# State-space inputs by four row groups with the power outermost, constants beside the memory's projection, and the angles' rounding constant added by ScalarE

## Time and profile before

| | |
|---|---|
| median of three runs | 4084.74 us |
| the profiled execution, its own time | 4090.44 us |
| its span on the core | 4089.1 us |
| TensorE busy, of the span | 3879.4 us, 95% |
| VectorE / ScalarE / GpSimd busy | 63% / 44% / 36% |
| mean granted TensorE clock | 0.969 of full speed |

### The profile page before, as it was taken

The page is one execution under the profiler, slowest core; times in us unless marked ns, Lnnn a source line. Parts: engine busy times, 40 slices in busy tenths (PEclk is TensorE's granted clock), DMA queues, the critical chain, the costliest instruction groups (busy, mean ns, idle before and its releaser), DMA issues.

```text
span 4089.1 us, 66513 instructions
## 1 busy us (share of the span) xinstructions
PE 3879.4 (95%) x28426; PEld 3308.2 (81%) x28426; DVE 2578.3 (63%) x3605; ACT 1794.3 (44%) x2785; POOL 1480.2 (36%) x701
## 2 busy tenths in 40 slices
PE   6898999999999999989899999999989989999998
PEld 3787888777877887888788888888978878888887
DVE  0435643795368897669678758784555966455457
ACT  1435443654355444445544444443334554333334
POOL 0332443143323440014334444445424434444443
PEclk8998999999999999999999999999689999999999
DMA  9653665345543451024346555556225435454543
GB/s 395 264 215 144 262 242 209 149 175 204 220 154 139 171 191 69 23 105 172 149 165 227 206 217 206 215 197 268 104 94 197 179 130 190 183 196 179 200 177 133
DMA packets 60119, 747.66 MB, mean 183 GB/s; under 512 B 6704, under 2 KB 8880, under 8 KB 16176
## 3 DMA queue, kind: packets, MB, share of 16 engines
q1 hardware_dynamic: 48960, 696.74, 44.7%
q0 software_dynamic: 8800, 44.57, 2.8%
q10 hardware_dynamic: 2064, 2.10, 0.1%
HBM read 726.60 MB, written 16.78 MB: 182 GB/s over the span
## 4 chain that ended last, share of the span: by engine, by line
PE 78%; DVE 12%; ACT 5%; DMA 3%; issue 1%; POOL 0%; another core or an unknown queue 0%; SPq 0%; DVEq 0%; ACTq 0%; POOLq 0%
PE ps L370 42%; PE ps L371 21%; DVE pieces L323 2%; PE ps L3548 2%; DMA ring<-in_ada 2%; PE ps L2229 2%; PE ps L790 2%; ACT pieces L307 2%; DVE r L1173 1%; DVE opa L571 1%; PE ps L1899 1%; DMA s5u<-in_s5bt 1%; PE ps L3578 1%; DVE scr L592 1%; PE ps L644 1%
## 5 line engine op out<-in xcount | busy, mean ns | idle before, releaser
L370 PE MATMUL ps<-opa,pieces 128*128 128x512 f32 x6192 | 2256.0, 407 | 59.4 <-DVE pieces L323 39.6
L341 POOL TENSOR_TENSOR pieces<-ring,pieces 128x1024 fp32r<-128x1024 f32 x539 | 1348.5, 2502 | 2233.9 <-ACT pieces L307 2224.2
L371 PE MATMUL ps<-opa,pieces 128*128 128x256 f32 x6192 | 1741.5, 281 | 0.0
L307 ACT ACTIVATE pieces<-ring 128x1024 fp32r<-128x1024 f32 (+1 forms) x1110 | 1098.4, 1036 | 838.3 <-PE ps L371 837.9
L370 PEld LDWEIGHTS ps<-opa,pieces 128*128 128x128 f32 x6192 | 1174.2, 190 | 355.8 <-issue 41.9
L371 PEld LDWEIGHTS ps<-opa,pieces 128*128 128x128 f32 x6192 | 1179.6, 191 | 9.0 <-issue 5.3
L370 PE MATMUL ps<-opb,pieces 128*128 128x512 f32 x2560 | 910.5, 397 | 18.6 <-DVE pieces L323 13.0
L323 DVE TENSOR_TENSOR pieces<-ring,pieces 128x1024 fp32r<-128x1024 f32 (+1 forms) x571 | 715.0, 1252 | 272.8 <-ACT pieces L307 269.3
L371 PE MATMUL ps<-opb,pieces 128*128 128x256 f32 x2560 | 726.0, 284 | 0.0
L370 PEld LDWEIGHTS ps<-opb,pieces 128*128 128x128 f32 x2560 | 483.4, 189 | 140.2 <-issue 15.3
L371 PEld LDWEIGHTS ps<-opb,pieces 128*128 128x128 f32 x2560 | 484.0, 189 | 0.1
(11 more groups left out here) (425 smaller groups left out, 3478.1 us busy)
## 6 DMA issues: line engine op xcount, KB each, us to landing
ring<-in_up SPq DMA_DIRECT2D x64, 2048.0 KB, 7.7
ring<-in_down SPq DMA_DIRECT2D x64, 2048.0 KB, 7.7
ring<-in_win SPq DMA_DIRECT2D x56, 2048.0 KB, 7.8
ring<-in_ada SPq DMA_DIRECT2D x48, 2048.0 KB, 12.1
ring<-in_wout SPq DMA_DIRECT2D x24, 2048.0 KB, 7.7
ring<-in_evin SPq DMA_DIRECT2D x18, 2048.0 KB, 7.8
ring<-in_evout SPq DMA_DIRECT2D x8, 2048.0 KB, 7.9
ring<-in_xkv SPq DMA_DIRECT2D x8, 2048.0 KB, 7.7
```

Of the source, the lines that this page charges most:

```text
L307: a.do.activation(K.parts_of(p)[0][:, s, :], w[:, s, :], ACT.Copy).then_inc(*K.hi.up((p, h)))
L341: g.do.tensor_tensor(lo[:, s, :], w[:, s, :], hi[:, s, :].bitcast(F), ALU.subtract).then_inc(*K.lo2.up(p))
L370: pe.do.matmul(b[:, 0:512], hi[:, k, :], op[:, 512 * k:512 * k + 512], start=i == 0, stop=False)
L371: t = pe.do.matmul(b[:, 0:256], lo[:, k, :], half(op, 0, k), start=False, stop=i == kt - 1)
```

## The change

The inputs `z5` of an s are computed in one call by all four row groups, with the power r outermost. VectorE's steps therefore wait for whole sets of four. The order of inputs and outputs on TensorE and of the output additions on VectorE is changed. The generators for the columns move from the first quarter's up tiles to the eight tiles of the memory's projection (`xkv`) of layer 0. `row5` is no longer made by `wide5` and matmuls: TensorE transposes the two 128x64 tiles, ScalarE copies the result, and it goes to HBM and comes back in 16 DMAs issued by GpSimd, each of 16 partitions with 16 repeats of 256 bytes. The load of the first table moves with it. ScalarE makes the second of the four angle operations. The pads of table 6 are spread over eight tiles.

```diff
@@ xattn, layer 0 @@
     for n in range(8):
+        if l == 0 and n == 6:
+            pe_s5_rows(K)
         side = pe_xvturn(K, l, n - 5) if n > 4 else None
@@ act_xattn / dve_xattn @@
+    columns = iter(()) if l else act_s5_columns(K)
     for n in range(8):
         act_feed(K, ahead(K, p + n))
+        next(columns, None)
...
+    columns = iter(()) if l else dve_s5_columns(K)
     for n in range(8):
         dve_feed(K, ahead(K, p + n))
         dve_normed(...)
+        for _ in range(1 + (n > 0)):
+            next(columns, None)
@@ pool_xo @@
     pool_feed(K, K.first["xo", l] - 1)
+    if l == 0:
+        pool_s5_first(K)
+        pool_s5_rows(K)
@@ pe_ffn @@
-            if l == 0 and q == 0 and n in (12, 15):
-                pe_s5_rows(K, n // 2 - 6)
@@ act_s5_columns: the four L3135 and the four L3142 go @@
+    a.wait_ge(*K.prod.of("lamT"))
+    a.do.activation(K.lamT, K.bank["lamT"][0:64, 0:256], ACT.Copy).then_inc(*K.act.up("lamT"))
@@ pe_s5_rows @@
+    for c, lam in enumerate((K.lre5, K.lim5)):
+        pe.wait_ge(*K.dve.of(("lam5", c)))
+        t = pe.do.transpose(b[0:64, P * c:P * c + P], lam, K.ident)
@@ new @@
+def pool_s5_rows_back(K):
+    g = K.g
+    g.wait_ge(*K.load["lamT"].of("lamT"))
+    g.wait_ge(*K.tile.of(K.first["up", 0, 0]))
+    for c in range(2):
+        for r in range(4):
+            for q in range(2):
+                at = 32 * r + 16 * q
+                rows = K.D["s5lam"].rearrange("(m r) (c q t) -> r c q m t", r=4, c=2, q=2)[r, c, q]
+                g.do.dma_start(K.row5[c][at:at + 16, :].rearrange("p (m t) -> p m t", m=16),
+                               rows[None].broadcast_to([16, 16, 64])).then_inc(*K.load["row5"].up("row5", 16))
@@ pool_s5_beside @@
     for t in range(2, 128):
+        if t == 4:
+            pool_s5_rows_back(K)
@@ act_s5_pads @@
-        yield
+            if j == 6:
+                yield
+        if j < 6:
+            yield
@@ pool_s5_angle / act @@
-    g.do.tensor_scalar(K.at5, K.aq, 1.0, MAG, ALU.mult, ALU.add).then_inc(*K.gps.up())
-    g.wait_ge(*K.gps.now())
+    g.wait_ge(*K.act.of(("whole5", m)))
     g.do.tensor_scalar(K.at5, K.at5, -MAG, None, ALU.add).then_inc(*K.gps.up())
+def act_s5_whole(K, m):
+    K.a.wait_ge(*K.gps.of(("turn5", m)))
+    K.a.do.activation(K.at5, K.aq, ACT.Copy, scale=1.0, bias=MAG).then_inc(*K.act.up(("whole5", m)))
@@ act_s5 @@
     for n in range(3, 16):
+        if n % 2 == 0:
+            act_s5_whole(K, n // 2)
         act_s5_tables(K, n)
@@ pe_s5 @@
-    pe_s5_in(K, 1, 0)
-    pe_s5_in(K, 1, 1)
+    pe_s5_in(K, 1)
     for s in range(4):
-        for h in range(2):
-            pe_s5_out(K, s, h)
-            if s < 2:
-                pe_s5_in(K, s + 2, h)
+        pe_s5_out(K, s, 0)
+        if s < 2:
+            pe_s5_in(K, s + 2)
+        pe_s5_out(K, s, 1)
@@ pe_s5_in @@
-    for m in range(4):
-        for c in range(2):
-            for r in range(4):
-                for q in qs:
+    for r in range(4):
+        for m in range(4):
+            for c in range(2):
+                for q in range(4):
                     q0 = 32 * q
@@ dve_s5 @@
-            v.wait_ge(*K.prod.of(("z5", n // 2 * 2 + 1)))
+            v.wait_ge(*K.prod.of(("z5", n // 4 * 4 + 3)))
...
-        if n >= 6 and n % 4 in (2, 3):
-            ... outputs (n - 6) // 4 * 4 + 2 * (n % 4 - 2) and the next
+        if n in (7, 11, 15):
+            outputs n - 7 and n - 6
+        if n in (10, 14):
+            outputs n - 8 and n - 7
         yield
-    for i in range(12, 16):
+    for i in range(10, 16):
         dve_s5_out(K, i)
```

More of the change, by code:

```diff
@@ L3053, in dve_ffn @@
     v = K.v
-    columns, tables = (iter(()), iter(())) if l else (dve_s5_columns(K), dve_s5_beside(K))
+    tables = iter(()) if l else dve_s5_beside(K)
     for q in range(4):
@@ L3066, in dve_ffn @@
             dve_part(K, K.opb, ("ho", l, q), n, s)
-            if n >= 2:
-                next(columns, None)
         p = K.first["down", l, q]
@@ L3117, in act_s5_columns @@
     dt, lr, x, th, ex, ph2, sh, d1, r, em, r2 = K.t5c
+    a.wait_ge(*K.dve.of(("nmem", 0, "h", 15)))
     a.do.activation(dt, K.col("ldt"), ACT.Exp).then_inc(*K.act.up("dt"))
-    for _ in range(5):
+    for _ in range(2):
         yield
@@ L3222, in dve_s5_table @@
         v.wait_ge(*K.load["s5c"].of("s5c"))
+        v.wait_ge(*K.load["lamT"].of("lamT"))
         v.wait_ge(*K.dve.of("fi"))
@@ L3228, in dve_s5_table @@
         a, b = (r3(K.row5[c], g) for c in range(2))
-        for c in range(2):
-            v.wait_ge(*K.act.of(("row5", c, 1)))
+        v.wait_ge(*K.load["row5"].of("row5"))
     if j == 4:
@@ L3260, in act_s5_pads @@
             a.wait_ge(*K.kept[u % 2].of(("kept", u - 2)))
-        else:
-            a.wait_ge(*K.prod.of(("row5", 1, 1)))
         to = K.pad5[u % 2]
@@ L3271, in act_s5_pads, with pe_s5_rows, pool_s5_rows @@
             a.do.activation(o, i, ACT.Copy, scale=K.half5[which == "b"][:, q:q + 1]).then_inc(*K.act.up(("pad", u)))
-        yield
-def pe_s5_rows(K, c):
-    pe = K.pe
-    pe.wait_ge(*K.act.of(("wide5", c)))
-    pe.wait_ge(*K.dve.of("fold5"))
-    for h in range(2):
-        b, was = K.xb.take(K.act, ("row5", c, h))
-        K.bank["row5", c, h] = b
-        pe.wait_ge(*was)
-        for m in range(8 * h, 8 * h + 8):
-            t = pe.do.matmul(b[:, 64 * (m - 8 * h):64 * (m - 8 * h) + 64], K.wide5[:, P * m:P * m + P], K.fold5, start=True, stop=True)
-        t.then_inc(*K.prod.up(("row5", c, h)))
+            if j == 6:
+                yield
+        if j < 6:
+            yield
+def pe_s5_rows(K):
+    pe = K.pe
+    b, was = K.xb.take(K.act, "lamT")
+    K.bank["lamT"] = b
+    pe.wait_ge(*was)
+    for c, lam in enumerate((K.lre5, K.lim5)):
+        pe.wait_ge(*K.dve.of(("lam5", c)))
+        t = pe.do.transpose(b[0:64, P * c:P * c + P], lam, K.ident)
+    t.then_inc(*K.prod.up("lamT"))
+def pool_s5_rows(K):
+    g = K.g
+    g.wait_ge(*K.act.of("lamT"))
+    g.do.dma_start(K.D["s5lam"], K.lamT).then_inc(*K.load["lamT"].up("lamT", 16))
+def pool_s5_rows_back(K):
+    g = K.g
+    g.wait_ge(*K.load["lamT"].of("lamT"))
[7 more added lines that the diff above has]
+                               rows[None].broadcast_to([16, 16, 64])).then_inc(*K.load["row5"].up("row5", 16))
 def act_s5_beside(K):
-    yield from beside(act_s5_columns(K), *(delayed(pads_from(j), act_s5_pads(K, j)) for j in range(7)))
+    yield from beside(*(delayed(pads_from(j), act_s5_pads(K, j)) for j in range(7)))
 def dve_s5_beside(K):
@@ L3325, in pool_s5_beside @@
     g, p = K.g, K.first["up", 0, 0]
-    store = {pads_from(u // 4) + u % 4 + 2: u for u in range(28)}
+    store = {pads_from(u // 4) + u % 4 * (1 + (u >= 24)) + 2 + (u >= 24): u for u in range(28)}
     for t in range(2, 128):
+        if t == 4:
+            pool_s5_rows_back(K)
         if t in store:
@@ L3338, in pool_s5_first @@
     g = K.g
-    g.wait_ge(*K.tile.of(K.first["xo", 0]))
+    g.wait_ge(*K.dve.of(("nmem", 0, "h", 15)))
     g.do.dma_start(K.T5[0], K.D["s5cc"]).then_inc(*K.load["s5c"].up("s5c", 16))
@@ L3424, in pe_odin @@
             K.pe.wait_ge(*K.act.of(("K", 0)))
-            pe_s5_in(K, 0, 0)
-            pe_s5_in(K, 0, 1)
+            pe_s5_in(K, 0)
 def pe_s5_direct(K, s):
@@ L3492, in pool_s5_angle @@
     turn = of_step(K.ph5, 2 * m, 2)[:, :, :, None].broadcast_to([P, 2, 4, 64])
-    g.do.tensor_tensor(K.aq.rearrange("p (d m k) -> p d m k", d=2, m=4), four, turn, ALU.mult).then_inc(*K.gps.up())
-    g.wait_ge(*K.gps.now())
-    g.do.tensor_scalar(K.at5, K.aq, 1.0, MAG, ALU.mult, ALU.add).then_inc(*K.gps.up())
-    g.wait_ge(*K.gps.now())
+    g.do.tensor_tensor(K.aq.rearrange("p (d m k) -> p d m k", d=2, m=4), four, turn, ALU.mult).then_inc(*K.gps.up(("turn5", m)))
+    g.wait_ge(*K.act.of(("whole5", m)))
     g.do.tensor_scalar(K.at5, K.at5, -MAG, None, ALU.add).then_inc(*K.gps.up())
```

44 lines of the change are left out of this document (16 added, 28 removed).

## The result

The changed kernel took 4042.93 us in the median of its first runs (4036.16 to 4049.95) against 4085.2 us (4084.2 to 4085.68) for four runs of the kernel before (the forecast started from 4084.74, the median of three of them): a ratio of 0.9897, 95% interval 0.9875 to 0.9919. The forecast was 4042 us. The profiled execution of the changed kernel took 4037.2 us (span 4035.9); that of the kernel before, 4090.44 (span 4089.1).

The account below looks back on a forecast made before the run. TensorE, busy 95% of the span, was taken as the bound. −13.0 −24 +0.6 −11.2 +1 +4.4 = −42.2 us from 4090.44 gave about 4048 profiled, 4042 us for the median; 8 in 10 within 4026 to 4066.

Parts of the forecast that it names:

- the step on the clock: In `pe_s5_in(0)`: full clock for 4.0 us, then half, so 10.0 us instead of 23.0; 13.0 us saved; forecast's mechanism 0.42.
- not side by side: Rival, four-row-group inputs: a round takes 224 ns, a set 22 us, in(0) saves nothing; 4087.5 us; chance 0.10.
- the clock stays up: Rival, four-group inputs: clock not falling saves 5.3 us more at inputs 0, 6 more in the stage; 4031 us; chance 0.28.
- the walk: State-space stage after odin, stepped through with the old durations: last product at 2991.6 instead of 3019.05, 27.4 us earlier.
- −24 was forecast: State-space stage after odin: 27.4 us from stepping through it, less 3 us for unexplained issue waits; 24 us saved.
- TensorE being short of instructions: Stage's end: 3 us taken off the gain for issue waits; as a rival 6 us more, 4048 us, chance 0.08.
- 3200 records at the 28 ns of a four-group round leave no room to catch up: Reason given for the rival of scarce TensorE instructions at the stage's end: 6 us more, 4048 us, chance 0.08.
- The waits that I named: In the stage: TensorE idle before out(0,0), released by GpSimd, and before in(3), released by the B table's DMA.
- the cost stays: Rival, up tiles: table loads or VectorE's scaling hold the columns' cost there; 11 us less saved, 4053 us; chance 0.04.
- That meeting: Beside the memory's projection: VectorE's half of the pieces starts later and meets GpSimd's; 1 us lost, bounds 0.5 and 4.
- dear issues: Rival, 16 DMAs at t = 4: GpSimd's issues cost 1.21 us each, 9.8 us more; 4052 us; chance 0.08.
- Rounding constant and table 6: Constant on ScalarE: 0.6 us lost, bounds 1 gained to 7 lost; table 6 over eight tiles: 0, bounds 5 gained.

## Why the prediction came out

The number was right, and the step on the clock that the forecast gave its largest chance was not. Two terms of the stage were wrong and cancelled. So that the median came within 1 us was luck, and a repeat on another chip gained 36.5 us instead of 42.3. What held was that four row groups run side by side, and by it the size of the gain.

*Four row groups side by side:* right. A set took 7.4 us at full clock (7.2 worked out) and 13.6 at half (13.6). The rival "not side by side" falls. The Trainium skill (TensorE: Matmul & The Clock Gate, on packing small matmuls) gives 3.07 times for four groups (with 512 moving columns), by which a set would take 9.3 us as an estimate; the 7.1 to 7.4 us of in(0) in every profile with four groups say that here, with 64, it was four times the pace of the full-height matmul's 115 ns.

*The clock:* the step "I take the present behaviour: full for 4.0 us, half for the other 28 rounds" failed. The forecast gave it 0.42; the rival "the clock stays up" had 0.28 and was what the trace showed in in(0), every time: 7.4 us, not 10.0. With two row groups in the new loop it fell after 3.9 us again. So in in(0) it was the number of row groups at work that kept it up, as that rival argued. Four groups don't keep it up everywhere: in in(1), which begins behind waits of 1.8 and 2.4 us, it fell 0.4 us after the start, so that the set took 13.6 us where the walk had 10; in in(3) it changed from one execution to the next. The odin tile behind in(0) was 2.1 us shorter at full clock (11.5 us from in(0)'s end to VectorE's next sum, 13.6 before), near the 2.5 that the rival gave it, but 0.7 of this was left at in(1)'s start, behind the wait for B of 1.

*The stage:* −24 was forecast and −24.1 measured, by other terms. The walk gave 27.4 us, or 33 with the clock up. From it I took 3 us for TensorE being short of instructions. That term is the one mis-sized: the waits for issue were 24.3 us, against 6.3 before and 4.8 in the row that I took it from. "3200 records at the 28 ns of a four-group round leave no room to catch up" was the right reason (delivery is 29.3 ns a matmul), but I gave it 6 us more and a chance of 0.08. What I missed is that out(s, h) itself asks for matmuls at 15 ns, so that the whole end of the stage goes by delivery. The waits that I named came only in part: the one for GpSimd before out(0,0) did (6.6 us); the one for B of 3 before in(3) did not, as TensorE was later than the table; one for B of 1 did before in(1) (2.4 us), which I had not seen. (The walk also has 4 MB for C of 2 and B of 3; the DMA view has 2048 and 1536 KB.)

*The columns:* they left the up tiles with all of their 11.2 us, so the rival "the cost stays" falls. Beside the memory's projection they cost 3.0 instead of 1, within the bounds. VectorE's timeline of the changed kernel there, and then GpSimd's:

```profile
1943.42 1.22 DVE L323 TENSOR_TENSOR pieces<-ring,pieces 128x1024 fp32r<-128x1024 f32 x1
...
1947.68 0.15 DVE L3155 TENSOR_SCALAR s5u<-cols 128x1 f32<-128x1 f32 x1
1947.76 3.45 DVE L323 TENSOR_TENSOR pieces<-ring,pieces 128x1024 fp32r<-128x1024 f32 x1
1951.13 0.68 DVE L382 TENSOR_REDUCE xa<-ps 128x256 f32<-128x512 f32 x1
...
1947.73 2.40 POOL L341 TENSOR_TENSOR pieces<-ring,pieces 128x1024 fp32r<-128x1024 f32 x1 [4.76 <-ACT pieces L307]
```

The small operations delay the pieces until they fall beside GpSimd's, and then the same operation takes 3.45 us instead of 1.22. That meeting was named in the forecast; its size was not.

*The 16 DMAs:* 8.94 us of GpSimd against 9.6, and 5.4 against 4.4 us on the path; "dear issues" (1.21 us each) falls. The Trainium skill (DMA: Bandwidth & Descriptors, Anatomy of one DMA) lets many descriptors be emitted before their cost shows, and the 0.56 us for 256 runs agrees.

*Rounding constant and table 6:* 0.6 and 0 forecast, nothing measurable and 0 found.

## What to carry to other kernels

Matmuls that fill only 32 rows go side by side by four row groups as well as by two, in either of the two orders of loops tried. In in(0) TensorE's clock stayed up with four where with two it fell; behind pauses it fell with four as well. Once they go side by side, count TensorE's instructions: where a profile shows waits for "issue" at every 128th matmul, the two changes of order tried here (the power innermost, in(2) ahead) brought nothing, but fewer matmuls did, even if two other engines must add for it. A wait that fills with work at half clock can cost more than it held.

## What the hardware showed that was not expected

- In a long run of short matmuls TensorE got 128 with their loads (256 instructions, one packet of the instruction queue) every 3.75 us, 29.3 ns a matmul. Short ones (15 ns each) stand still for 1.2 to 2.1 us after every 128. The 256 of in(0), behind a stretch of larger matmuls, came in 7.4 us without such a gap.
- Where this met the loads of the tables, two gaps were 3.3 to 4.2 us long in each profile with whole sets of inputs and all output products in place but one (the inputs alone in the kernel before, which had one), always at the same places of the code; that it is the traffic which lengthens them was not tried.
- An operation of VectorE on 128x1024 took 1.22 us alone, 3.45 beside GpSimd's piece, and 7.78 beside 16 DMA issues and the pieces behind them. By the rows above it stood beside the issues for 2.0 us without coming to its end and beside the pieces for 4.7. In both cases it ended 1.1 us after GpSimd's pieces, which is about its time alone: it did little or nothing while GpSimd was at work.
- The clock in in(3) was at its upper level (granted 1.00) in one profile of the changed kernel and at the lower (0.50) in another: some 5 us that nothing in the program explains so far.
